# A layer of mLSTM mixer and SwiGLU: a new order of units in the second norm, and two pairs' row sums moved from GpSimd to VectorE

## What is computed

```
u = rmsnorm(x) * mix_norm_g
h = x + mlstm_mixer(u)            # 8 heads, chunkwise scan, gated, then @ w_out (1024 x 1024)
u = rmsnorm(h) * ffn_norm_g
out = h + (silu(u @ w_gate) * (u @ w_up)) @ w_down      # D_FF = 2816
```

## Time and profile before

| what | value |
|---|---|
| profiled execution: its own time | 2248.88 us |
| its span, first to last instruction | 2247.2 us |
| TensorE busy | 2169.3 us, 97% |
| VectorE busy | 1459.4 us, 65% |
| ScalarE busy | 922.8 us, 41% |
| GpSimd busy | 282.3 us, 13% |
| mean granted TensorE clock | 0.988 |
| chain that ended last | TensorE 87%, VectorE 7%, issue 2%, DMA 2%, ScalarE 2% |

### The profile page before, as it was taken

The page is one execution under the profiler, slowest core; times in us unless marked ns, Lnnn a source line. Parts: engine busy times, 40 slices in busy tenths (PEclk is TensorE's granted clock), DMA queues, the critical chain, the costliest instruction groups (busy, mean ns, idle before and its releaser), DMA issues.

```text
span 2247.2 us, 29481 instructions
## 1 busy us (share of the span) xinstructions
PE 2169.3 (97%) x10440; PEld 1779.8 (79%) x10440; DVE 1459.4 (65%) x2274; ACT 922.8 (41%) x1670; POOL 282.3 (13%) x373
## 2 busy tenths in 40 slices
PE   5999989989999999999989999799899999999999
PEld 4788878878888888888868888688688888888887
DVE  8765467786656565578677644667765656656764
ACT  4433653344333333345434346433433333333443
POOL 4111111120101010100112111111210100100000
PEclk9999999999999999999999999999999999999999
DMA  4333354213232323863414334532123233257443
GB/s 142 99 113 108 105 214 141 85 47 113 99 112 89 107 95 133 300 220 113 150 61 136 99 99 146 206 132 76 55 97 108 96 102 101 93 200 239 146 128 107
DMA packets 200289, 281.56 MB, mean 125 GB/s; under 512 B 12913, under 2 KB 131697, under 8 KB 200177
## 3 DMA queue, kind: packets, MB, share of 16 engines
q1 hardware_dynamic: 171696, 183.07, 25.4%
q0 software_dynamic: 28480, 97.02, 12.3%
HBM read 197.73 MB, written 82.31 MB: 125 GB/s over the span
## 4 chain that ended last, share of the span: by engine, by line
PE 87%; DVE 7%; issue 2%; DMA 2%; ACT 2%; SPq 0%; POOL 0%; DVEq 0%; ACTq 0%; POOLq 0%
PE ps L2163 13%; PE ps L2165 13%; PE ps L2166 13%; PE ps L1912 7%; PE ps L1916 6%; PE ps L1914 6%; PE ps L2209 6%; PE ps L2213 6%; PE ps L2211 6%; PE ps L1825 2%; PE ps L1826 2%; PE ps L1827 2%; PE ps L1832 1%; DMA vtc<-proj_hbm 1%; PE ps L2082 1%
## 5 line engine op out<-in xcount | busy, mean ns | idle before, releaser
L1666 DVE TENSOR_TENSOR ring<-raw_f,ring 128x512 fp32r<-128x512 f32 x308 | 211.4, 687 | 196.8 <-ACT ring L1103 196.3
L1103 ACT CAST ring<-raw_f 128x512 fp32r<-128x512 f32 x308 | 190.4, 622 | 215.4 <-PE ps L2166 200.5
L2163 PE MATMUL ps<-u_lo,ring 128*128 128x512 f32 x704 | 277.6, 394 | 0.0
L2165 PE MATMUL ps<-u_hi,ring 128*128 128x512 f32 x704 | 276.1, 392 | 0.0
L2166 PE MATMUL ps<-u_hi,ring 128*128 128x512 f32 x704 | 275.8, 392 | 0.0
L2209 PE MATMUL ps<-ring,ring 128*128 128x512 f32 x616 | 244.4, 397 | 3.0 <-DVE ring L1744 2.9
L2213 PE MATMUL ps<-ring,ring 128*128 128x512 f32 x616 | 243.5, 395 | 0.0
L2211 PE MATMUL ps<-ring,ring 128*128 128x512 f32 x616 | 243.5, 395 | 0.0
L2163 PE MATMUL ps<-t_op,ring 128*128 128x512 f32 x528 | 208.7, 395 | 6.2 <-DVE ring L1666 6.2
L2166 PE MATMUL ps<-t_op,ring 128*128 128x512 f32 x528 | 209.0, 396 | 0.0
L2165 PE MATMUL ps<-t_op,ring 128*128 128x512 f32 x528 | 208.6, 395 | 0.0
(11 more groups left out here) (219 smaller groups left out, 4263.7 us busy)
## 6 DMA issues: line engine op xcount, KB each, us to landing
ops_hbm<-kept POOLq DMA_DIRECT2D x154, 256.0 KB, 2.4
g_in<-ops_hbm SPq DMA_DIRECT2D x154, 256.0 KB, 2.7
raw<-in_ml_w_in_dram SPq DMA_DIRECT2D x24, 1024.0 KB, 5.3
proj_hbm<-pkept POOLq DMA_DIRECT2D x96, 256.0 KB, 2.7
raw_f<-in_ffn_w_gate_dram SPq DMA_DIRECT2D x44, 512.0 KB, 4.6
raw_f<-in_ffn_w_up_dram SPq DMA_DIRECT2D x44, 512.0 KB, 4.5
b<-in_ffn_w_down_dram SPq DMA_DIRECT2D x88, 256.0 KB, 4.9
x_in<-in_x_dram SPq DMA_DIRECT2D x16, 512.0 KB, 5.9
```

The source lines that it names most:

```text
L1103: nc.scalar.copy(four(ring[slot][:, 0, :]), feed_source(q, s)).then_inc(w_hi_done, 1)
L1666: nc.vector.tensor_tensor(four(ring[slot][:, 1, :]), feed_source(q, s), four(ring[slot][:, 0, :].bitcast(F32)), ALU.subtract).then_inc(w_l ...
L2163: pe.matmul(banks(bank), wh, moved(kind, 1, k), start=(fresh and k == 0), stop=False, skip_group_check=True)
L2165: pe.matmul(banks(bank), wh, moved(kind, 0, k), start=False, stop=False, skip_group_check=True)
```

## The change

Cut to its core. `made_at` and `made_pool_at` only count semaphore steps anew, since VectorE now makes four row sums for pairs 0 and 1 of the second norm. The region that holds the `hg` tiles grows from 32 KB + 128 to 32 KB + 512 bytes, and the third `hg` tile moves by 384 bytes.

```diff
+SECOND_UNITS = [("B", 0), ("A", 0), ("B", 1), ("A", 1), ("B", 2), ("B", 3), ("A", 2), ("A", 3), ("C", 0), ("C", 1),
+                ("C", 2), ("C", 3)]
+def all_on_vector(stage, p):
+    return stage % 2 == 1 and p < 2
@@ SyncE, start of the scan
                 load_og(0)
+                load_vtc(2)
+                load_qkc(2)
                 load_og(1)
+                load_wo(1, 0)
                 sp.wait_ge(colt_turned, h + 1)
                 sp.dma_start(gain2[:, :], ...)
-                load_wo(1, 0)
                 load_wo(1, 1)
-                for c in range(2, TILES):
+                load_og(2)
+                for c in range(3, TILES):
@@ GpSimd
-                pool.wait_ge(p_stored[1], h * 384 + 384)
-                nc.gpsimd.memset(v1[1][:, :, DV:VW], 1.0).then_inc(ones_set, 1)
-                pool.wait_ge(p_fed, h * PU + PU)
-                load_res(0)
                 def squares(c):
...
                     nc.gpsimd.tensor_tensor(hrow[:, :, :], num[:, :, 0:DV], num[:, :, 0:DV], ALU.mult)\
                         .then_inc(sq_done, 1)
-                    if 1 <= c < 4:
+                    if c == 0:
+                        pool.wait_ge(p_stored[1], h * 384 + 384)
+                        nc.gpsimd.memset(v1[1][:, :, DV:VW], 1.0).then_inc(ones_set, 1)
+                        pool.wait_ge(p_fed, h * PU + PU)
+                    if c < 4:
                         load_res(c)
...
                 store_h(5)
-                sum_late(st + 1, 0)
                 store_h(6)
-                sum_late(st + 1, 1)
                 sum_late(st + 1, 2)
@@ ScalarE, scan: split_out(1, 0..3) in one run behind head_rstd(1); 4, 5 before keep_num(2); 6, 7 behind head_rstd(2)
@@ ScalarE, second norm
                 feed_hi(0, 3)
-                for n in range(5, OP_UNITS):
+                for n in range(5, 10):
                     op_hi(st + 1, n)
+                feed_hi(0, 4)
                 first_kept(0)
+                feed_hi(0, 5)
                 first_kept(1)
-                feed_hi(0, 4)
-                feed_hi(0, 5)
+                op_hi(st + 1, 10)
+                op_hi(st + 1, 11)
                 feed_hi(0, 6)
@@ ScalarE and VectorE, group 0: op_hi / op_lo(st + 1, 12 + q) behind feed_hi / feed_lo(0, q + RING), q < 4
@@ VectorE, sum_early
+                if all_on_vector(stage, p):
+                    nc.vector.tensor_tensor(late[:, 0:NB], late[:, NB:D], late[:, 0:NB], ALU.subtract)\
+                        .then_inc(t_made, 1)
+                    dve.wait_ge(t_made, made_at(stage, p) + 2)
+                    nc.vector.tensor_tensor(early[:, NB:D], early[:, NB:D], t2r, ALU.subtract).then_inc(t_made, 1)
@@ VectorE, scan, c = 1 and 2: add_out(c - 1, 0) now ahead of all four split_out(1, 4c - 4 .. 4c - 1)
@@ VectorE, second norm
                 gate_heads(7)
+                sum_early(st + 1, 0)
                 hg_low(7)
                 norm2_rows(5)
                 add_out(6, 1)
-                sum_early(st + 1, 0)
                 sum_early(st + 1, 1)
                 norm2_rows(6)
-                add_out(7, 0)
                 op_lo(st + 1, 0)
                 op_lo(st + 1, 1)
+                add_out(7, 0)
                 sum_early(st + 1, 2)
                 op_lo(st + 1, 2)
+                add_out(7, 1)
                 op_lo(st + 1, 3)
-                add_out(7, 1)
                 op_lo(st + 1, 4)
                 norm2_rows(7)
                 feed_low(0, 3)
                 op_lo(st + 1, 5)
                 sum_early(st + 1, 3)
-                for n in range(6, 10): ... feed_sums(0, 2) ... 10 to 13 ... feed_sums(0, 3) ... 14, 15 ... feed_lo(0, 4 to 6)
+                op_lo 6, 7, feed_sums(0, 2), op_lo 8, feed_sums(0, 3), op_lo 9, feed_lo 4, feed_lo 5, op_lo 10, 11, feed_lo 6
@@ TensorE, turn_unit: for pairs 0 and 1, parts B and C wait for t_made (made + 3, made + 4), not for t_made_pool
@@ TensorE
-                out_tile(7, 1, 0, 4)
+                out_tile(7, 1, 0, 6)
                 turn_unit(st + 1, 3)
-                out_tile(7, 1, 4, KD)
+                out_tile(7, 1, 6, KD)
                 turn_unit(st + 1, 4)
@@ TensorE, feed_group
                         if first and q == 4:
-                            turn_unit(st + 1, 13)
-                            turn_unit(st + 1, 14)
-                            turn_unit(st + 1, 15)
-                            pe.wait_ge(op_lo_done, (st + 1) * OP_UNITS + OP_UNITS - 2)
+                            pe.wait_ge(op_lo_done, (st + 1) * OP_UNITS + 10)
                         if first and q == 6:
-                            pe.wait_ge(op_lo_done, (st + 1) * OP_UNITS + OP_UNITS - 1)
+                            pe.wait_ge(op_lo_done, (st + 1) * OP_UNITS + 12)
+                        if first and 4 <= q < 7:
+                            feed(n, q, b, 0, 2)
+                            turn_unit(st + 1, 9 + q)
+                            feed(n, q, b, 2, 4)
+                            continue
```

More of the change, by code:

```diff
@@ L111, in out_at, with made_at, made_pool_at @@
     return h * 16 + OUT_ORDER.index((c, jj)) + 1
+def all_on_vector(stage, p):
+    return stage % 2 == 1 and p < 2
+def made_at(stage, p):
+    return 20 * (stage // 2) + (2 * p if stage % 2 == 0 else 8 + (4 * p if p < 2 else 4 + 2 * p))
+def made_pool_at(stage, p):
+    return 12 * (stage // 2) + (2 * p if stage % 2 == 0 else 4 + 2 * p)
 def made_of(i, part=0):
@@ L151, in mlstm_layer @@
         r_v = region(TILES * HEADS * VW * 4)
-        r_q = region(32 * KB + P)
+        r_q = region(32 * KB + 512)
         r_a = region(16 * KB)
@@ L193, in mlstm_layer @@
         num = place("num", r_c + 28 * KB, [P, HEADS, VW], F32)
-        hg_at = [r_q, r_q + 8 * KB, r_q + 24 * KB + P]
+        hg_at = [r_q, r_q + 8 * KB, r_q + 24 * KB + 512]
         hg_hi = [place(f"hg_hi{s}", at, [P, KD, P], F32R) for s, at in enumerate(hg_at)]
@@ L400, in part_of @@
         def part_of(stage, n):
-            return FIRST_UNITS[n - 4][0] if stage % 2 == 0 else "BAC"[(n - 4) % 3]
+            return (SECOND_UNITS if stage % 2 else FIRST_UNITS)[n - 4][0]
         def pair_of(stage, n):
-            return FIRST_UNITS[n - 4][1] if stage % 2 == 0 else (n - 4) // 3
+            return (SECOND_UNITS if stage % 2 else FIRST_UNITS)[n - 4][1]
         def unit_bank(stage, n):
@@ L631, in _ @@
                         sp.wait_ge(turned, 2 * (h + 1) * OP_UNITS + 1)
-                        sp.wait_ge(t_made_pool, 2 * (h + 1) * 8 + 2)
+                        sp.wait_ge(t_made_pool, made_pool_at(2 * (h + 1), 1))
                         load_x(h + 1, 7)
@@ L668, in sum_late @@
                 _, t2r, t4r = t_rows(stage, p)
-                made = stage * 8 + 2 * p
+                made = made_at(stage, p)
                 pool.wait_ge(t_made, made + 1)
@@ L948, in _ @@
                 proj_hi(h, 4)
-                act.wait_ge(t_made_pool, st * 8 + 8)
+                act.wait_ge(t_made_pool, made_pool_at(st, 4))
                 op_hi(st, 9)
@@ L1075, in _ @@
                         act.wait_ge(p_fed, h * PU + PU)
-                    if c in (1, 2):
-                        split_out(1, 4 * c - 4)
-                        split_out(1, 4 * c - 3)
+                    if c == 2:
+                        split_out(1, 4)
+                        split_out(1, 5)
                     if c >= 3:
@@ L1086, in _ @@
                     head_rstd(c)
-                    if c in (1, 2):
-                        split_out(1, 4 * c - 2)
-                        split_out(1, 4 * c - 1)
+                    for k in ((), range(0, 4), range(6, 8))[c] if c < 3 else ():
+                        split_out(1, k)
                 def feed_hi(n, q):
@@ L1198, in feed_group @@
                             feed_hi(n, q + RING)
+                            if isinstance(n, int) and n == 0 and q < 4:
+                                op_hi(st + 1, 12 + q)
                         elif not last:
@@ L1253, in sum_early @@
                 nc.vector.tensor_tensor(t1r, late[:, 0:NB], early[:, 0:NB], ALU.subtract).then_inc(t_made, 1)
-                dve.wait_ge(t_made, stage * 8 + 2 * p + 1)
+                dve.wait_ge(t_made, made_at(stage, p) + 1)
                 nc.vector.tensor_tensor(t2r, late[:, NB:D], t1r, ALU.subtract).then_inc(t_made, 1)
+                if all_on_vector(stage, p):
[3 more added lines that the diff above has]
+                    nc.vector.tensor_tensor(early[:, NB:D], early[:, NB:D], t2r, ALU.subtract).then_inc(t_made, 1)
             def op_lo(stage, n):
@@ L1440, in _ @@
                     proj_lo(0, 4)
-                    dve.wait_ge(t_made_pool, st * 8 + 8)
+                    dve.wait_ge(t_made_pool, made_pool_at(st, 4))
                     op_lo(0, 9)
@@ L1634, in _ @@
                     if c in (1, 2):
-                        split_out(1, 4 * c - 2)
-                        split_out(1, 4 * c - 1)
+                        for k in range(4 * c - 4, 4 * c):
```

(30 more changed lines are left out.)

3 lines of the change are left out of this document (removed).

## The result

The changed kernel takes 2195.05 us, the median of four runs (2190.81 to 2199.62), beside 2248.3 us for the kernel before (four runs, 2246.48 to 2250.45). The ratio is 0.976, with a 95% interval of 0.974 to 0.979. The profiled execution took 2194.73 us, its span is 2193.0 us and its mean granted clock 0.993.

What follows compares the result with a forecast made beforehand. TensorE, busy 97% of the span, was taken as the bound, gaining only from fewer waits and less half clock. 2.0 + 3.1 + 11.3 = 16.4 us a half, 32.8 together, gave 2216.2, stated as 2217 us; range 2211 to 2229.

Steps and rivals of the forecast that it cites:

- The moved 384 bytes: Third hg tile's shift: claimed to cost nothing that any row shows, with 1 us allowed either way.
- Squares: Chunk 0 of the scan: GpSimd's squares ahead of the store's wait bring turn_heads(0) 2.0 us earlier a half.
- `vtc`, 3.1 us: Chunks 1 and 2: vtc 2 early in the queue removes TensorE's wait; the stage gains 3.1 us a half, not 5.
- the two new ones: New TensorE waits around turn_heads(1): about 1.3 us before it and 1.2 us behind it.
- the wait for `wo`: Chunk 3: the 1.8 us wait for the last piece of wo[1] was to stay.
- the feared 1.5 us of half clock: Chunks 1 and 2: up to 1.5 us lost if the waits near turn_heads(1) bring the half clock.
- The norm, 11.3 us: Second norm: fewer waits and less half clock, less new waits, save 11.7 us a half, taken as 11.3.
- The subtractions on VectorE: Second norm, pairs 0 and 1: first four take 2.6 us, with 2 us of cover, nothing paid; all meet no GpSimd work.
- (a): Rival: VectorE's handover bounds the norm, eight units 0.7 us late, 5.6 us a half; 2228 us, chance 0.13.
- (b): Rival: the scan's edits give nothing, 10.2 us less gain; 2227 us, chance 0.11.
- (c): Rival: slower, TensorE at half clock from product 0 to 6 of the norm, 25 us a half; 2267 us, chance 0.03.
- (d): Rival: a wait on an old count holds a unit, the norm keeps its time; 2239 us, chance 0.05.

Runs made afterwards that it cites:

- a_noalign: The changed kernel with only the region and the third hg tile put back at 32 KB + 128 bytes: 2218.10 us, ratio 0.987.
- b_norm: The kernel before plus the 512 bytes and the second norm's edits, without the scan's edits: 2204.98 us, ratio 0.980.
- a_pool: The changed kernel with T3 and T4 of pairs 0 and 1 of the second norm on GpSimd again: 2195.35 us, ratio 0.977.
- b_scan: The kernel before plus the 512 bytes and the scan's edits (vtc 2 and qkc 2 early, squares earlier, later wo[1] pieces): 2214.12 us, ratio 0.986.
- b_align: The kernel before with only the hg region at 32 KB + 512 bytes and its third tile moved, order of work untouched: 2227.49 us, ratio 0.991.
- a_off64: The changed kernel with the hg region 64 bytes longer, so all tiles behind it lie 64 bytes off: 2218.43 us, ratio 0.987.
- a_off32: The changed kernel with the hg region 32 bytes longer, so all tiles behind it lie 32 bytes off: 2220.95 us, ratio 0.988.

## Why the prediction was right, and where it failed

**The failed step** is "The moved 384 bytes cost nothing that any row shows; either way I allow 1 us." They brought 21 to 23 us of a gain of 53, as much as the whole of the norm's new order (22.5). Behind it stands a choice of the first part, to take the matmul's pace (0.235 and 0.23 us) as a property of TensorE that a change can't touch. Without this term the forecast holds: `a_noalign` has 2218.1 us against 2217. That it is met to 1 us is luck, since the time itself is known only to some 3 us and the parts measured one by one (4.9, 1.8 and 11.3, so 18.0 a half) come to more than the 16.4 of the sum.

**Squares, 2.0 us forecast.** `hrow`'s wait went from 6.38 to 4.30, with ScalarE late as foreseen: `head_rstd(0)` moved by 2.1 us beyond the 2.9 that the whole timeline had moved. The times of the runs have 1.8 us, with an error as large as itself. The lower clock came after the wait, as said, but for a shorter stretch.

**`vtc`, 3.1 us.** The wait is gone and the two new ones stand where they were placed: 0.80 (forecast 1.3) and 1.07 (1.2); the wait for `wo` stays (1.85, forecast 1.8). `outputs(2)` moved from 334.02 to 325.25, that is 8.77, less 2.86 and 2.07 that came from ahead of it: 3.84 us. The runs say 4.9, to about 2.5, so they don't tell 3.1 from it. In the trace the term that was off is the new waits, together 0.6 us too dear; the feared 1.5 us of half clock did not come.

**The norm, 11.3 us.** Counted from `turn_heads(7)` (451.69 before, 442.46 after, so 9.23 is added to times of after): `hg_low(7)` at 457.45 (forecast 457.4), `op_lo(0)` 467.46 (467.4), product 0 474.66 (474.7) behind a wait of 1.11 (1.3), unit 12 492.71 (492.7) behind 0.56 (0.6), the start of product 7 (which was at 514.41) at 502.82, against the forecast end of product 6 at 502.7. Unit 3 stands directly behind `out_tile` with no wait. The stage from `turn_heads(7)` to there shrank from 62.72 to 51.13 us (forecast: about 51), that is 11.6, of which the faster pace has some tenths; `b_norm` has 11.3.

The subtractions on VectorE were forecast to be free, and they are. But the sentence on the two engines in each other's way read as if something were won by it. The Trainium skill, "SBUF — State Buffer", section "Who interferes with whom", says that such a pair takes turns at a port. `a_pool` agrees in the durations (1.97 in place of 1.22 us) and shows that the time doesn't follow, since VectorE waits for ScalarE behind them.

**Rivals.** (a) did not occur: no unit was late beyond those two waits, though VectorE, busy 15.07 of 16 us there, has little room left. (b) is refuted by `b_scan`, 13.4 us below `b_align`. (c), slower, is refuted by the window 453 to 492 at a granted clock of 1.00. For it spoke what the Trainium skill, "TensorE: Matmul & The Clock Gate", section "Part 4: PE-mode transpose", says of transposes and the clock; in this mix of transposes and matmuls the trace does not bear that rule out. (d) is refuted by `b_norm`, 22.5 us below it. None of the rivals held the case that came: a change in the speed of work that the diff doesn't touch. The range was built from rivals of the schedule alone, so its lower end, 2211, had nothing under it.

## What to carry to other kernels

When a diff moves a buffer's address, even by a few hundred bytes in passing, split the long matmul lines of the trace by product and compare start-to-start times before costing the move at nothing; a pace that differs between products of the same shape is a term that the move can change. On this kernel, laying every tile that meets in a matmul out at the same distance modulo 256 bytes was worth as much as all of the norm's rescheduling. What it brings elsewhere isn't measured here. Moving work off an engine that stretches another pays only if that other is what the path waits for.

## What was not expected of the hardware

- A 128x512 matmul in a steady row starts every 226.7 ns where all weight tiles and moving tiles lie level modulo 256 bytes, and the down products, whose two tiles are 32, 64 or 128 bytes off, every 232 to 233 ns. Feed products that are off take 228 to 233 ns, and a level one behind them up to 231. Moving both tiles by 128 bytes changes nothing (2193.12 us against 2195.05).
- The level pace itself is 226.7 ns. The Trainium skill, "TensorE: Matmul & The Clock Gate", section "Wait — 56ns, not 53.3ns?", gives 215.7 ns for 512 columns on the warm clock; no run here showed that, and neither pace here is it.
- A part of the gain in pace comes back as waits: those for `ring` in the down products are 2.9 to 3.6 us in the kernels that are off (before, `a_noalign`, `a_off64`, `a_off32`) and 3.7 to 7.9 us in the level ones (3.7 in `b_scan`, 6.1 after, 7.9 in `b_align`).
